# A streaming hybrid layer on one core: denser gate and projection products, and an expert combine that is added up in memory

## The reference, cut to what matters

```
adaLN(c) -> RMSNorm -> one combined input projection -> three token mixers
  A: gated linear attention   B: gated DeltaNet (delta rule, chunks of 64)
  C: S5 diagonal complex SSM: h_t = Lambda h_{t-1} + B u_t, y_t = Re(C h_t) + D u_t, GLU
-> per-branch projection -> per-channel sigmoid gates -> one output projection -> gated residual add
adaLN(c) -> RMSNorm -> MoE: top-1 of 4 groups, then top-2 of the 4 experts in it -> gated residual add
final RMSNorm
```

## Time and profile before

| | us |
|---|---|
| median of the runs | 2025.4 |
| the profiled execution, time | 2023.8 |
| its span | 2021.6 |
| TensorE busy | 1840.6 (91%) |
| VectorE busy | 847.2 (42%) |
| ScalarE busy | 433.2 (21%) |
| GpSimd busy | 197.7 (10%) |

### The profile page before, as it was taken

One profiled execution on the slowest core, in us unless ns is written; L12 is line 12 of the kernel. 1 busy time (PEld: TensorE's weight loads), 2 busy tenths in 40 slices (PEclk: granted clock), 3 DMA queues, 4 the chain that ended last, 5 costly groups with the idle time before them and its releaser, 6 DMA issues. The chain is left out here.

```text
span 2021.6 us, 29838 instructions
## 1 busy us (share of the span) xinstructions
PE 1840.6 (91%) x11953; PEld 1219.7 (60%) x11953; DVE 847.2 (42%) x1751; ACT 433.2 (21%) x858; POOL 197.7 (10%) x230
## 2 busy tenths in 40 slices
PE   6999988999998999999869999899999849999990
PEld 4575555665445688677459999678744435555550
DVE  3826741301107433455234544523333354454447
ACT  4221021003204111112121221401111113333322
POOL 2000000000000000111011111000000002222225
PEclk8999999999999999999879999999999969999995
DMA  9076533021003110111000000111431079877226
GB/s 313 28 103 186 188 107 107 0 47 42 0 16 64 32 32 11 43 22 31 11 23 13 2 13 13 47 45 32 145 131 42 26 265 313 286 256 265 84 77 272
DMA packets 143689, 188.73 MB, mean 93 GB/s; under 512 B 20912, under 2 KB 117800, under 8 KB 140376
## 3 DMA queue, kind: packets, MB, share of 16 engines
q1 hardware_dynamic: 129208, 155.70, 25.0%
q0 software_dynamic: 8112, 28.04, 4.1%
q10 hardware_dynamic: 6240, 3.15, 0.6%
HBM read 158.32 MB, written 27.37 MB: 92 GB/s over the span
## 5 line engine op out<-in xcount | busy, mean ns | idle before, releaser
L3179 PE MATMUL ex_ps<-ex_ring,ex_xt 128*64 x800 | 178.4, 382 | 2.6 <-DVE ex_xt L3273 2.6
L3180 PE MATMUL ex_ps<-ex_lane_in,ex_xt 128*64 128x256 f32 x800 | 178.4, 382 | 0.0
L3179 PEld LDWEIGHTS ex_ps<-ex_ring,ex_xt 128*64 128x64 f32 x800 | 110.3, 138 | 68.2 <-issue 17.8
L2738 PE MATMUL pj_ps<-w_out,mix 128*128 128x512 f32 (+1 forms) x288 | 126.7, 599 | 2.6 <-PEq L3352 2.6
L449 PE MATMUL fr_ps<-h,fr_w_gate 128*128 128x364 f32 (+1 forms) x384 | 121.9, 476 | 0.0
L3180 PEld LDWEIGHTS ex_ps<-ex_lane_in,ex_xt 128*64 128x64 f32 x800 | 110.3, 138 | 0.0
L449 PEld LDWEIGHTS fr_ps<-h,fr_w_gate 128*128 128x128 f32 x384 | 72.8, 192 | 50.7 <-issue 10.0
L3199 PE MATMUL ex_ps<-ex_ring,ex_inner_t 128*64 x200 | 93.2, 610 | 6.6 <-issue 6.6
L2738 PEld LDWEIGHTS pj_ps<-w_out,mix 128*128 128x128 f32 (+1 forms) x288 | 53.0, 186 | 71.0 <-issue 71.0
L1721 PE MATMUL cv_ps<-h,late 128*128 128x364 f32 (+1 forms) x288 | 92.1, 482 | 3.0 <-PEq L3352 3.0
L3200 PE MATMUL ex_ps<-ex_lane_down,ex_inner_t 128*64 128x512 f32 x200 | 93.3, 610 | 0.0
(11 more groups left out here) (628 smaller groups left out, 3234.7 us busy)
## 6 DMA issues: line engine op xcount, KB each, us to landing
fr_y_cols<-in_w_ada SPq DMA_DIRECT2D x8, 2048.0 KB, 7.7
ex_ring<-in_w_exp_gate SPq DMA_DIRECT2D x16, 1024.0 KB, 5.6
ex_ring<-in_w_exp_up SPq DMA_DIRECT2D x16, 1024.0 KB, 10.4
ex_ring<-in_w_exp_down SPq DMA_DIRECT2D x16, 1024.0 KB, 12.7
ex_ring<-ys_dram SPq DMA_DIRECT2D x8, 1024.0 KB, 12.7
mix<-in_x_prompt SPq DMA_DIRECT2D x8, 512.0 KB, 11.5
glu_w_br<-in_w_ada SPq DMA_DIRECT2D x4, 1024.0 KB, 13.8
branch<-in_w_in SPq DMA_DIRECT2D x2, 2048.0 KB, 14.3
```

What stands on the lines that cost most here:

```text
L2738: last = nc.tensor.matmul(ps[2 * (i % 2) + c][0:n], g.mix[:, k, P * i:P * i + n], w[:, k, 512 * c:512 * c + 512], start=k == 0, stop=k == ...
L3179: nc.tensor.matmul(bank[A, 0:FF], xt[:, s % 2, k, A], own, start=k == 0, stop=k == KD - 1, skip_group_check=True)
L3180: last = nc.tensor.matmul(bank[B, 0:FF], xt[:, s % 2, k, B], lane_in[:, s % 2, k, f], start=k == 0, stop=k == KD - 1, skip_group_check=True)
```

## The change

1. **Front.** `MOD` uses four column strips. The scan is split in eight segments of 16 blocks, which VectorE advances side by side; then the carries between segments are worked out, and each segment gets its share of the carry by powers of the step: 96 dependent instructions in place of 384, and a table of powers ahead. `EARLY` is 6, so two gate groups (j = 6 and 7) stand behind the S5 output rounds, and SyncE issues the load of `glu_w` after the scan.
2. **Delta rule.** The gate is made transposed: the slab of the weight is stationary and a piece of 364 tokens moves. 12 jobs of eight products, each cut in shares of three, three and two, at the same four places of an iteration. The w-k products go head by head, with the two row halves in turn.
3. **Output stage.** VectorE normalises in nine instructions, TensorE transposes between the gate pieces, and VectorE multiplies gate, channel scale and the transposed rows straight from PSUM in nine more; ScalarE's copies go.
4. **Projection.** Tiles (2,3), (4,5) and (6,7) are done as pairs by seven block products in place of eight (sums and differences of half matrices, made by VectorE). Projection runs three tiles ahead. Each x1 tile is also stored to `ys_dram`, one row per token.
5. **Experts.** `row_home` holds the token's own row. Each slot is scattered in two halves of 64 rows that are added to what is in memory: the second issued when the first has landed, since a token may be in both lanes. `gates_of` waits for both. At the end SyncE reads one row per token, which already is the sum; the adds of GpSimd and VectorE are gone.

```
-        MOD = [(32 * (c % 3), c // 3) for c in range(8)]
+        MOD = [(32 * (c % 4), c // 4) for c in range(8)]
-        EARLY = 7
+        EARLY = 6
+        SEG = 16
+        NSEG = NBP // SEG
...
-            for b in range(NBS):
-                advance(before[:, :, :, b:b + NBP + 1:NBP], before[:, :, :, b + 1:b + NBP + 2:NBP], True, 3 * b)
-            with dve.Fori(0, 17) as r:
...
+            for j in range(SEG - 1):
+                width = NSEG + 1 if j < NBS else NSEG
+                advance(starts(j, width), starts(j + 1, width), g.s5_step[:], width)
+            out = product(starts(SEG - 1, NSEG - 1), g.s5_step[:], NSEG - 1)
+            then(nc.vector.tensor_tensor(carry, out[:, 0], out[:, 1, ::-1], ALU.add))
+            for q in range(1, NSEG - 1):
+                advance(carry[:, :, :, q - 1:q], carry[:, :, :, q:q + 1], seg_step, 1)
+            for q in range(1, NSEG):
...
+                then(nc.vector.tensor_tensor(whole_seg, whole_seg, share[0], ALU.add))
+                then(nc.vector.tensor_tensor(whole_seg, whole_seg, share[1][:, ::-1], ALU.add))
...
-        JOBS = [(c, t) for c in range(BR // P) for t in range(NT)]
+        JOBS = [(c, n) for c in range(KB) for n in range(3)]
+        PLACES = 4
+        SHARES = ((0, 3), (3, 6), (6, KD))
...
-                    last = nc.tensor.matmul(ps[7][:, q], g.h[:, k, P * t:P * t + P], w_gate[:, c % 2, k], start=q == 0 and k == 0,
...
+                for k in range(*SHARES[share]):
+                    last = nc.tensor.matmul(gate_ps[:, 0:width], w_gate[:, c % 2, k], g.h[:, k, at:at + width], start=k == 0, stop=k == KD - 1,
...
-                for c, bank in enumerate((2, 0)):
-                    for h in range(HEADS):
+                for h in range(HEADS):
+                    for c, bank in enumerate((2, 0)):
...
+        PLAIN, PAIR_TILES = (0, 1, NT - 1), ((2, 3), (4, 5), (6, 7))
+        AHEAD = 3
...
+                sp.wait_ge(S["added"], i + 1)
+                sp.dma_start(g.ys_dram[P * i:P * i + n, :], x1[0:n, i]).then_inc(S["x1_stored"], 16)
...
-                nc.gpsimd.indirect_dma_start(g.ys_dram, bass.IndirectOffsetOnAxis(ap=g.row_home[:, s:s + 1], axis=0), y[:], None).then_inc(S["stored"], 16)
...
+                for half, lane in enumerate((A, B)):
+                    if s or half:
+                        pool.wait_ge(S["stored"], 32 * s + 16 * half)
+                    nc.gpsimd.indirect_dma_start(g.ys_dram, bass.IndirectOffsetOnAxis(ap=g.row_home[:, half, s:s + 1], axis=0), y[lane], None,
+                                                 compute_op=ALU.add).then_inc(S["stored"], 16)
...
-                    dve.wait_ge(S["stored"], 16 * s)
+                    dve.wait_ge(S["stored"], 32 * s)
...
-                sp.dma_start(rows[i][0:size(i)], g.ys_dram[2 * P * i:2 * (P * i + size(i)), :].rearrange("(t k) c -> t k c", k=2)).then_inc(rows_in[i], 16)
+                sp.dma_start(x1[0:size(i), i], g.ys_dram[P * i:P * i + size(i), :]).then_inc(rows_in[i], 16)
```

More of the change, by code:

```diff
@@ L775, in _ @@
-            for b in range(NBS):
-                advance(before[:, :, :, b:b + NBP + 1:NBP], before[:, :, :, b + 1:b + NBP + 2:NBP], True, 3 * b)
-            with dve.Fori(0, 17) as r:
[L778 to L781, removed]
+            scanned = [0]
@@ new lines, in advance, with starts @@
+            def advance(now, nxt, step, width):
+                out = product(now, step, width)
+                then(nc.vector.tensor_tensor(nxt, nxt, out[:, 0], ALU.add))
+                then(nc.vector.tensor_tensor(nxt, nxt, out[:, 1, ::-1], ALU.add))
+            def starts(j, width):
+                return before[:, :, :, j:j + SEG * (width - 1) + 1:SEG]
+            for j in range(SEG - 1):
+                width = NSEG + 1 if j < NBS else NSEG
+                advance(starts(j, width), starts(j + 1, width), g.s5_step[:], width)
@@ L2106, in copy, with gates_out @@
                 nc.scalar.activation(to, of, ACT.Copy).then_inc(S[name], 1)
[L2108 to L2113, removed]
+            def gates_out(i, q):
+                job, share = divmod(PLACES * i + q, 3)
+                if share < 2:
+                    return
+                c, n = JOBS[job]
+                at, width = PIECES[n]
+                act.wait_ge(S["gate_psum"], job + 1)
+                if job == len(JOBS) - 1:
+                    act.wait_ge(g.conv_stored, 32)
+                nc.scalar.activation(g.branch[:, c, at:at + width], gate_ps[:, 0:width], ACT.Copy).then_inc(S["gate_out"], 1)
             act.wait_ge(S["pre_psum"], 1)
@@ L2748, in _ @@
             pe.wait_ge(S["w_loaded"], 32)
-            project(0)
-            project(1)
+            for i in range(AHEAD):
+                project(i)
             pe.wait_ge(S["route_loaded"], 64)
@@ L2826, in _ @@
                 nc.vector.tensor_tensor(h2[:, i % 3], h2[:, i % 3], rows[:, 2, who], ALU.add).then_inc(S["h2"], 1)
-                if i >= 1:
-                    logit(i - 1)
-                if i + 1 < NT:
-                    add_branches(i + 1)
-            logit(NT - 1)
+            add_branches(0)
+            normalise(0)
+            sums_of_tokens(0)
+            add_branches(1)
+            normalise(1)
+            for pair, (one, two) in enumerate(PAIR_TILES):
+                add_pair(pair)
+                logit(2 * pair)
+                normalise(one)
+                normalise(two)
+            add_branches(NT - 1)
+            logit(NT - 4)
+            normalise(NT - 1)
+            for i in range(NT - 3, NT):
+                logit(i)
             dve.wait_ge(S["logit_turned"], 1)
```

366 lines of the change are left out of this document (251 added, 115 removed).

## The result

The changed kernel takes 2041.84 us (median of 4 runs, 2040.12 to 2045.39), before 2025.73 in the same comparison: ratio 1.0082, 95% interval 1.0061 to 1.0103. It is slower by 16 us; the forecast was 2025, no change. The profiled execution has a span of 2038.3 us against 2021.6, 16.7 more.

What follows compares the result with a forecast made beforehand. TensorE was taken as the bound nearly everywhere except the last 52 us. From 2023.8 us, savings of 60.5 and scatters costing 60 gave 2023.3, with 1.6 to the median 2025 us; range 1970 to 2105.

Steps and rivals of the forecast that it cites:

- forecast case: Whole kernel: no change that matters, two large terms of opposite sign; chance 0.45, own range 1995 to 2055 us.
- LA + LB + 3.2: Expert slot chain in us: landing times of first and second half scatter, plus 3.2 for issue, refill and multiplies.
- threshold of 9.1 us: Expert slots: TensorE's 12.32 us period holds while the two half scatters' landing times sum to under 9.1 us.
- price of an added half: Expert stage: priced as one plain 128-row scatter, median 4.7 us with weights loaded, 8.5 while they load.
- Loaded slots: Expert slots meeting a weight load: 17.9 us each, 5.6 over TensorE's, 11 of them, 62 us in all.
- rival 1: Expert stage: added rows cost more than copied ones; 2055 us at 1 us more per scatter, 2116 at 2; chance 0.27.
- Rival 2: Expert stage: half the rows land in much less; 1983 us, or 1965 if loads miss y; chance 0.20.
- Rival 3: Delta rule and projection: VectorE's or ScalarE's chains cut TensorE's savings by 15 to 20 us; 2043 us; chance 0.08.
- Front: First stage: fewer modulation passes, a shorter scan and moved gate pieces take 14 us less (4 to 18).
- Delta rule: Delta-rule stage: gate jobs save 11 us and reordered w-k products 3, together 14 less (0 to 18).
- Projection: Projection stage: fewer block products save 10.4 us, some extra sums show, so 8.5 less (0 to 10.4).
- Tail: After the last slot's scatter: 29.8 us in place of 52.4, so 22 less (15 to 26).

Runs made afterwards that it cites:

- plain_halves: The changed kernel with the two half scatters overwriting instead of adding, all waits kept, output lacking the sum: 1984.52 us, ratio 0.9804.
- light_loads: The changed kernel with experts from the fifth on loading only an eighth of gate and up and a quarter of down: 2008.88 us, ratio 0.9928.
- no_accumulate: The changed kernel with the routing, experts and tail of before, and without the store of x1 to ys_dram: 1983.26 us, ratio 0.9796.
- wk_old: no_accumulate with the delta rule's w-k products in the order of before, one row half for all heads, then the other: 1985.66 us, ratio 0.9822.
- only_accumulate: The kernel of before with the changed routing, experts and tail, and the store of x1 that they need: 2078.92 us, ratio 1.0281.
- two_regions: The changed kernel with the second half scatter added into another memory region, issued right behind the first, output incomplete: 1977.01 us, ratio 0.9776.

## Why the prediction was wrong, step by step

The sign was not forecast; the time, 2042, lies in the forecast case's own range. The mechanism was right: LA + LB + 3.2 through the one buffer y, a threshold of 9.1 us, TensorE's gains whole, a shorter tail. What failed is one term, the price of an added half; the other misses in the table have both signs and nearly cancel, which is luck.

- **The step that failed**: "Half the rows, with a read of the old row more, I price as one such scatter", and from it that in quiet slots LA + LB gives "a chain of 11.2 to 12.6: about free, 1 us in all". From issue to issue A takes 6.47, and B 4.73 to the refill, the chain 14.07. plain_halves shows that the price was right for two plain halves (11.12), and that the add comes on top with 1.5 us each. The twelve slots that no load makes longer are 18.7 us over TensorE's where I had 1: that accounts for the 16 by which the slots' 76.1 pass the forecast's 60, and it is as large as the miss in the time. With the loads made small (light_loads) the 24 slots are 43 over.
- **Loaded slots**: forecast 11 at 5.6 over TensorE's, 62; measured twelve at 4.8, 57.4. That this came near is in part luck: the 10 that I took for A was near a plain scatter's worst landing of 10.7, and the add filled what it had to spare (beside a load A takes mostly 9.2 to 10.1 with the add, 8.3 to 9.2 without it in plain_halves). In four of the twelve it was B that met the load's start, not A.
- **The rivals**: what came is the mechanism of rival 1, with its sign (quiet slots over 13 us). Its sum is wrong: 1 us more for each scatter makes the quiet chain 13.2 to 14.6, some 20 us over in 13 slots and not 8, so about 2067 in place of 2055; and the 22 that it adds to the loaded slots did not come. Rival 2 (halves land quicker) fails on plain_halves: 64 rows take as long as 128. Rival 3 (TensorE's savings hidden) fails on no_accumulate: all 41 us are there.
- **Front**: -16 against -14. The output rounds start at 253.96, 28 earlier; ScalarE's copies still hold them up by 5.10, as said, and the next stage starts 1.77 behind the last product in place of 5.22.
- **Delta rule**: -7.5 against -14. I took a gate job at 5.02 from an uncut row; cut in three it takes 2.03 + 2.03 + 1.41 = 5.47, so 5.7 us are gained and not 11. The w-k products are 4.4 less in busy time (I had 3), and wk_old's stage is 3.5 longer without this. The other 2.5 us are spread over small groups and were not followed up.
- **Projection**: -9.7 against -8.5. **Output stage**: -0.9 against -2.
- **Unforecast**: 6 us less in three stages between, which the change hardly touches. Their instructions are the same; the granted clock in the GLU stage is 1.00 against 0.97 before. only_accumulate, which has the old front, takes 91.5 in the GLU stage, as before, and the changed kernel 89.0, so that part comes with the new front; why is not shown.
- **Tail**: -17 against -22. The two scatters took 9.5 (2002.89 to 2012.38) and not 7.2: the same add again (A to B 4.88 here, 3.48 in plain_halves). The first half megabyte took 3.7 (3.5 forecast), the rest 3 more than I had.

## What to carry to other kernels

Price a chain of small dependent transfers per transfer, not per byte: here halving the rows saved nothing, and the add put 1.5 us on each. Before a producer's single buffer gets a second round trip, compare round trips plus refill with the period of the engine that sets the pace, and give the buffer a twin if the sum is over it. And an edit that pays in one place and loses in another is best run as its two halves: here a gain of 2.0% and a loss of 2.8% stood behind a loss of 0.8%.

## What the runs showed of the hardware

- A plain scatter of 64 rows of 4 KB lands in the time of one of 128 (4.73 us in plain_halves, 4.7 before, weights loaded, VectorE's copy beside both).
- An accumulating scatter costs GpSimd 1.42 us to issue, a plain one 0.89, for the same 64 rows.
- Two accumulating scatters to different memory, issued one behind the other, overlap: a slot takes 11.46 us with two_regions, 14.07 with B issued when A has landed.
